# Routing weights as two scaled float16 parts instead of three bfloat16 parts

## The reference

```python
def peer(h, w_q, subkeys, u_tab, v_tab):      # 16384 experts, 8 heads, 16 chosen per head
    q = (xb @ w_q).reshape(PEER_BLOCK, PEER_HEADS, PEER_QDIM)
    s1, s2 = ...                              # scores of the two halves against 128 keys each
    v1, i1 = lax.top_k(s1, PEER_TOPK)
    v2, i2 = lax.top_k(s2, PEER_TOPK)
    cs, ci = lax.top_k(cand, PEER_TOPK)       # cand: all 16 x 16 sums
    e = i1[ci // 16] * PEER_N_KEYS + i2[ci % 16]
    g = jax.nn.softmax(cs, axis=-1)
    a = jax.nn.gelu(einsum('pd,phkd->phk', xb, u_tab[e]), approximate=False)
    return einsum('phk,phkd->pd', g * a, v_tab[e])
```

## Time and profile before

| | |
|---|---|
| time, median of 3 runs | 2585.95 us (2585.71 to 2589.53) |
| span of the profiled execution, its own time | 2591.7 us |
| PE busy | 2514.7 us, 97% |
| DVE busy | 2119.7 us, 82% |
| ACT busy | 1220.0 us, 47% |
| POOL busy | 468.9 us, 18% |
| PE in the routing products L1948 | 111.8 us, 3072 instructions |
| granted TensorE clock, mean | 0.990 |

### The profile page before, as it was taken

How to read it: one execution, slowest core, us unless ns; L and a number is a source line. 1 busy time by engine, 2 the same in 40 slices (tenths; PEclk the granted TensorE clock), 3 DMA queues, 4 the chain that set the end, 5 groups by cost and what they waited for, 6 DMA issues and landing times.

```text
span 2591.7 us, 48983 instructions
## 1 busy us (share of the span) xinstructions
PE 2514.7 (97%) x17184; PEld 2192.0 (85%) x17184; DVE 2119.7 (82%) x3783; ACT 1220.0 (47%) x1769; POOL 468.9 (18%) x385
## 2 busy tenths in 40 slices
PE   5999999999999999999999999999999999999998
PEld 4789999888888877899998888887878789777987
DVE  7889997888888778869978888887777788777754
ACT  4544444545444545444444554444545554334543
POOL 2115992000000001018980000000101000110000
PEclk8999999999999999999999999999999999999999
DMA  9775555555456887365555445546887567964554
GB/s 345 259 263 168 179 178 172 166 166 185 169 167 211 284 271 272 130 220 171 183 179 166 162 166 185 170 168 231 282 286 256 189 222 262 318 242 163 171 183 149
DMA packets 147831, 538.38 MB, mean 208 GB/s; under 512 B 16609, under 2 KB 16865, under 8 KB 147442
## 3 DMA queue, kind: packets, MB, share of 16 engines
q1 hardware_dynamic: 114226, 414.78, 46.9%
q0 software_dynamic: 32752, 119.24, 13.2%
q10 hardware_dynamic: 720, 2.62, 0.3%
HBM read 533.42 MB, written 3.15 MB: 207 GB/s over the span
## 4 chain that ended last, share of the span: by engine, by line
PE 83%; DVE 7%; POOL 3%; issue 3%; DMA 2%; ACT 2%; SPq 0%; DVEq 0%; POOLq 0%; ACTq 0%
PE ps L2003 26%; PE ps L1529 9%; PE ps L2748 7%; PE ps L748 6%; PE ps L1505 6%; PE ps L1457 5%; PE ps L1533 5%; PE ps L2730 5%; PE ps L1948 3%; PE ps L1509 3%; POOL split_lo L1575 3%; PE ps L2734 2%; DVE gate L928 1%; DMA gate<-in_mod 1%; PE ps L2142 1%
## 5 line engine op out<-in xcount | busy, mean ns | idle before, releaser
L1562 ACT ACTIVATE split_hi<-ring 128x1024 fp32r<-128x1024 f32 x760 | 801.0, 1056 | 757.8 <-PE ps L1509 199.8
L1587 DVE TENSOR_TENSOR split_lo<-ring,split_hi 128x1024 fp32r<-128x1024 f32 x572 | 698.5, 1222 | 177.0 <-ACT split_hi L1562 172.2
L1575 POOL TENSOR_TENSOR split_lo<-ring,split_hi 128x1024 fp32r<-128x1024 f32 x128 | 339.9, 2672 | 91.2 <-ACT split_hi L1562 90.9
L1559 ACT ACTIVATE gate_hi<-gate 128x256 fp32r (+1 forms) x252 | 105.4, 418 | 405.4 <-PE ps L2003 398.9
L2003 PE MATMUL ps<-split_hi,gate_hi 128*128 128x512 f32 x1024 | 285.1, 398 | 1.5 <-DVE gate_lo L1585 1.5
L2003 PE MATMUL ps<-split_hi,gate_lo 128*128 128x512 f32 x1024 | 278.2, 392 | 5.1 <-DVE gate_lo L1585 5.0
L2003 PE MATMUL ps<-split_lo,gate_hi 128*128 128x512 f32 x1024 | 278.0, 391 | 0.0
L1505 PE MATMUL ps<-h_parts,split_hi 128*128 128x256 f32 x2048 | 266.9, 283 | 0.0
L1529 PE MATMUL ps<-h_parts,split_hi 128*128 128x512 f32 x1024 | 261.6, 397 | 0.0
L1505 PEld LDWEIGHTS ps<-h_parts,split_hi 128*128 128x128 f32 x2048 | 254.9, 192 | 0.0
L2003 PEld LDWEIGHTS ps<-split_hi,gate_lo 128*128 128x128 f32 x1024 | 192.6, 189 | 48.4 <-DVE gate_lo L1585 7.5
(11 more groups left out here) (405 smaller groups left out, 3951.0 us busy)
## 6 DMA issues: line engine op xcount, KB each, us to landing
ring<-in_stream SPq DMA_DIRECT2D x776, 512.0 KB, 4.3
small<-in_mod POOLq DMA_DIRECT2D x104, 512.0 KB, 5.6
mod_w<-in_mod POOLq DMA_DIRECT2D x64, 512.0 KB, 5.2
gate<-in_mod POOLq DMA_DIRECT2D x44, 512.0 KB, 6.9
gate<-in_mod SPq DMA_DIRECT2D x8, 512.0 KB, 16.2
gate<-in_mod ACTq DMA_DIRECT2D x4, 512.0 KB, 8.3
x_kept<-x POOLq DMA_DIRECT2D x8, 256.0 KB, 3.9
gate<-x_kept POOLq DMA_DIRECT2D x4, 512.0 KB, 8.5
```

Source lines behind the costliest of these rows:

```text
L1562: nc.scalar.activation(split_hi[:, e, :], ring[:, slot, e * D:(e + 1) * D], ACT.Copy).then_inc(hi_made, 1)
L1575: nc.gpsimd.tensor_tensor(split_lo[:, e, :], ring[:, slot, e * D:(e + 1) * D], split_hi[:, e, :].bitcast(F32), ALU.subtract).then_inc(lo_m ...
L1587: nc.vector.tensor_tensor(split_lo[:, e, :], ring[:, (START[name] + j) % RING, e * D:(e + 1) * D], split_hi[:, e, :].bitcast(F32), ALU.sub ...
```

## The change

The routing weight is multiplied by 2^15 and split in two float16 parts of eleven bits each, where before it was split in three bfloat16 parts. Every marker, key and part buffer becomes float16 (same two bytes). `W_PARTS` goes from 3 to 2, so a group has 16 products, not 24, and VectorE multiplies two parts, not three. The factor 2^15 comes in as `w_left` is copied out of PSUM (a copy becomes a multiplication by a constant), and is taken out in the merge, where a tensor-tensor product becomes a scalar-tensor-tensor one.

```diff
-        W_PARTS = 3
+        W_PARTS, W_SCALE = 2, float(2 ** 15)
...
-            ap = B.take(n // 2).bitcast(BF16)
+            ap = B.take(n // 2).bitcast(FP16)
...
-                nc.vector.tensor_copy(w_left[:, i * P:(i + 1) * P], ps[:, 4 + i, 2 * P:3 * P]) \
+                nc.vector.tensor_scalar(w_left[:, i * P:(i + 1) * P], ps[:, 4 + i, 2 * P:3 * P], W_SCALE, None, ALU.mult) \
                     .then_inc(vector_steps, v.step(f"selT{l}"))
-            nc.vector.tensor_copy(keys_bf, iota[:, :]).then_inc(vector_steps, v.step())
+            nc.vector.tensor_copy(keys_half, iota[:, :]).then_inc(vector_steps, v.step())
...
-            nc.vector.tensor_tensor(dst, dst, ps[:, 5 + j % 2, :].rearrange("p (t n) -> p n t", t=8),
-                                    ALU.mult).then_inc(banks_free, 1)
+            nc.vector.scalar_tensor_tensor(out=dst, in0=ps[:, 5 + j % 2, :].rearrange("p (t n) -> p n t", t=8),
+                                           scalar=1.0 / W_SCALE, in1=dst, op0=ALU.mult, op1=ALU.mult) \
+                .then_inc(banks_free, 1)
```

More of the change, by code:

```diff
@@ L32 @@
 F32R = mybir.dt.float32r
-BF16 = mybir.dt.bfloat16
+FP16 = mybir.dt.float16
 P = 128
@@ L1426, in build, with take_fp16 @@
         GROUP = 8
-        W_PARTS = 3
-        def take_bf16(*shape):
+        W_PARTS, W_SCALE = 2, float(2 ** 15)
+        def take_fp16(*shape):
             n = int(np.prod(shape))
-            ap = B.take(n // 2).bitcast(BF16)
+            ap = B.take(n // 2).bitcast(FP16)
             return ap.rearrange("p (a b) -> p a b", a=shape[0]) if len(shape) == 2 else ap
         PAIR = 2
[L1434 to L1437, removed]
+        selT = take_fp16(2 + W_PARTS, SEQ * PAIR).rearrange("p n (t q) -> p n t q", q=PAIR)
+        keys_half = take_fp16(1, KEYS)[:, 0, :]
+        hot_c = [take_fp16(GROUP, KEYS) for _ in range(2)]
+        hot_r = [[take_fp16(GROUP, HALF) for _ in range(W_PARTS)] for _ in range(2)]
         w_left = B.take(SEQ)
@@ L1820, in of_key @@
             def of_key(k0, n):
-                return keys_bf[:, k0:k0 + n].rearrange("p (k q) -> p k q", q=PAIR).unsqueeze(1) \
+                return keys_half[:, k0:k0 + n].rearrange("p (k q) -> p k q", q=PAIR).unsqueeze(1) \
                     .to_broadcast([P, GROUP, n // PAIR, PAIR])
```

## The result

The changed kernel takes 2561.65 us (median of four runs, 2558.07 to 2570.53) against 2587.53 us (four runs) for the kernel before: 25.9 us faster. The recorded ratio is 0.9896, 95% interval 0.9873 to 0.9918 (the two medians alone give 0.9900). The forecast was 2554.9 us in a range of 2548 to 2562. The measured median lies in the range, 6.8 us above the forecast and 0.35 us inside the range's upper end. The interval is nearly 12 us wide, so what the forecast is worth has to be read from the trace.

The account below looks back on a forecast made before the run. TensorE was taken to bound the routed slabs. 30.3 us from 1024 fewer products plus 0.8 at the `v` pass starts made 31.1 us, off the median 2585.95 giving 2554.9 us; range for 8 in 10, 2548 to 2562.

Parts of the forecast that it names:

- Reading the bound: Routed slabs: everybody waits for TensorE and TensorE for nobody, so each microsecond taken from it there shortens the slab.
- 29.6 ns a product: Routing products on TensorE: distance between starts; 1024 products fewer at 29.6 ns give 30.3 us.
- The upper bound of 36.4: Routing products on TensorE: busy time over count, 36.4 ns each, so at most 37.3 us for the 1024 removed.
- The rival with 97 ns a pair: Routing products at L1949: float16 loads slower on TensorE, 108 us longer, 2694 us; chance 0.04.
- the rival of a 32-bit rate: Marker instructions: VectorE treats float16 at the 32-bit rate and becomes the bound, 25 us longer, 2611 us; chance 0.03.
- 0 to 0.07 more: Merge on VectorE as scalar-tensor-tensor: 0 to 0.07 us more a slab than 0.68, hidden by spare time.
- the rival of 1.36: Dearer merge: 1.36 us passes the `v` slab's spare by 0.22; 17 us of gain left, 2569 us; chance 0.04.
- The start of a `v` pass: Two groups back to back: TensorE's wait for VectorE's markers goes, 0.4 us in each of two layers, 0.8 us.
- The selection: Once a layer: last rounding (2.63 us) and a subtraction fall away; VectorE is ready sooner, worth nothing.
- Room in the `v` slab: Markers' lead over TensorE's need in a `v` slab: spare of 0.36 us becomes 0.46.
- The likeliest case: Whole kernel: the forecast gain arrives, 2551 to 2558 us; chance 0.86.
- half the way to a dearer merge: Upper end of the 8-in-10 range, 2562 us, set halfway to the rival in which the merge takes 1.36 us.

## Why the prediction was right

**Reading the bound.** Right: the slabs shortened as TensorE's work did, 6.38 to 6.14 us in `u` and 6.27 to 6.05 on the mean in `v`, and putting the products back (399.5 us) undid it.

**29.6 ns a product.** Right to 3%, and the term that mattered: 29.4 by the distance between starts in one slab, 28.7 and 28.9 by what the layer lost in the two steps from three parts to one. So the 1024 products were worth 29.4 us and not 30.3. The `u` slabs gave the 0.24 us of the forecast and the `v` slabs 0.22; why these gave less was not followed. The upper bound of 36.4 was wide because a busy share holds each group's tail.

The Trainium skill, "TensorE: Matmul & The Clock Gate", section "Part 1: The HAM clock gate", gives a start-to-start distance of the columns at 2.4 GHz plus about 2.5 ns. An estimate from it for 64 columns is 29.2 ns, and the 28.7 to 29.4 measured agree.

**Float16 loads.** The rival with 97 ns a pair is out: 16 float16 pairs take 0.47 us, and three float16 parts last as long as three bfloat16 parts (399.9 us).

The Trainium skill, "TensorE: Matmul & The Clock Gate", section "Weight-path perf modes — Fast Weight Load (FWL) and DoubleRow", has the fast load on for 128 weights of every input type but FP32. That float16 takes as long as bfloat16 agrees with it.

**Float16 on VectorE.** 0.41, 0.68 and 0.42 us, as bfloat16; the rival of a 32-bit rate is out. **The merge** takes 0.68 us, the lower end of 0 to 0.07 more, and the rival of 1.36 is out.

**The start of a `v` pass.** 0.4 us a layer, as forecast, shown by the kernel with only VectorE relieved, and again by the one with VectorE's product put back, where the wait returns.

**The selection** gave nothing, as forecast, but not because VectorE had only got rid of work. In the changed kernel:

```profile
400.01 2.63 POOL L1575 TENSOR_TENSOR split_lo<-ring,split_hi 128x1024 fp32r<-128x1024 f32 x1 [1.11 <-ACT split_hi L1562]
400.39 2.53 DVE L1831 TENSOR_TENSOR small<-small 128x512 f16<-128x512 f16 x1
...
402.88 2.91 POOL L1575 TENSOR_TENSOR split_lo<-ring,split_hi 128x1024 fp32r<-128x1024 f32 x1 [0.25 <-ACT split_hi L1562]
403.44 2.97 DVE L1837 TENSOR_TENSOR small<-small 128x512 f16<-128x512 f16 x2
```

In the kernel before, the slow instructions were the last rounding of the earlier trace rows, 2.63 us, and the subtraction ahead of it:

```profile
400.52 2.53 DVE L1787 TENSOR_TENSOR small<-small 128x256 f32<-128x256 f32 x1
```

Both are gone, and the first marker and a first product are now the slow ones, 2.53 and 2.63 us in place of 0.42. The first marker ends at 402.92, GpSimd's subtraction at 402.64, and the next pair at about 406.07 and 405.79: VectorE's instruction ends 0.28 us after GpSimd's, as if it had waited for it. The markers are ready at 406.41 and not 407.78, so VectorE won 1.4 us and not the 5 us of the two instructions; it made no difference since TensorE wants them at 408.09.

The Trainium skill, "SBUF — State Buffer", section "🔬 SBUF: two separate sides", describes a pair of ports that VectorE (in an instruction with two SBUF inputs) and GpSimd take by turns for a whole instruction each. The rows agree with it; no run here separates it from another cause.

**Room in the `v` slab.** The forecast was 0.46 us, and 0.44 to 0.49 were measured. What it would cost to pass it was mis-stated in the rival of the dearer merge, which charged the whole overrun; the runs with more work on VectorE show about half in the slabs, and a cost at the start of the pass that the rival did not have.

**The time.** The sum of 31.1 us is 30.2 in the routed part. The step that was too simple is the last one, that the rest of the program stays as it is: it took 1791.9 us before and 1799.3 in the first profile after, 1790.0 in another, with nothing changed in it. The runs of the changed kernel spread over 15 us, and the range of the forecast had no term for it. The miss of 6.8 us has three parts: 1.6 since the kernel before now has a median of 2587.53 and not 2585.95, 0.9 from the sum, and 4.3 that stand outside the routed part or are the spread of the runs.

That the measured median lies in the range at all was luck. The likeliest case alone spanned 2551 to 2558 us, and 2561.65 is above it. The range reached to 2562 only because half the way to a dearer merge was added, and the merge is no dearer: 0.68 us.

## What to carry to other kernels

When an engine is busy without a gap, price an instruction by the distance between starts in a run of its kind, and measure the change over the stretch that it touches: here the time from the first to the last group repeats to 0.1 us, while whole runs spread over more than 10. An engine that is off the path has two kinds of room, its idle time and the lead of its results, and passing the lead need not cost one for one: look for what releases the late engine, and whether the wait comes before or after that release. Untouched stages can take back a quarter of a gain in one execution (7.4 of 30.2 us) and nothing in the next.

## What was not expected of the hardware

- The same 96 products of 64 rows, behind the same 1.52 us of idle time, took 8.61 us in one execution and 14.82 in another of the same program. What decides it is open.
- Marker instructions of 0.42 us on VectorE took 2.53 and 2.63 us beside GpSimd's subtraction of 1024 elements, and the slow rate goes with the time, not with the instruction: other instructions at that place got it before the change. The timeline shows the order (each ends 0.28 us after GpSimd's); no run took GpSimd's work away.
- Behind 24 filling products in the attention stage the clock was at 2.4 GHz where it had fallen without them, and the values took 3.5 and not 6.9 us, but the filling products themselves cost most of that.
